# The last layer's gate columns of the modulation: the sum over weight blocks made by VectorE instead of TensorE

## What is computed

```python
s_lat = jax.nn.silu(c)
s_ctx = jax.nn.silu(c_ctx)
for l in range(DEPTH_2):
    last = l == DEPTH_2 - 1
    ...
    shift, scale, gate = jnp.split((s_lat @ w_mod[l] + b_mod[l])[:, None, :], 3, axis=-1)
    shift_c, scale_c, gate_c = jnp.split(s_ctx @ w_mod[l] + b_mod[l], 3, axis=-1)
    ...
    if not last:
        ...
        ctx = ctx + gate_c * y_c
    x = x + gate * y
```

## Time and profile before

| what | us |
|---|---|
| median of 3 runs | 2725.45 |
| lowest and highest run | 2723.93, 2725.97 |
| profiled execution | 2726.38 |
| its span | 2724.6 |
| TensorE busy | 2705.9 |
| VectorE busy | 1775.1 |
| ScalarE busy | 1299.4 |
| GpSimd busy | 337.6 |

### The profile page before, as it was taken

One profiled execution on the slowest core, in us unless ns is written; L12 is line 12 of the kernel. 1 busy time (PEld: TensorE's weight loads), 2 busy tenths in 40 slices (PEclk: granted clock), 3 DMA queues, 4 the chain that ended last, 5 costly groups with the idle time before them and its releaser, 6 DMA issues.

```text
span 2724.6 us, 32623 instructions
## 1 busy us (share of the span) xinstructions
PE 2705.9 (99%) x13110; PEld 2138.1 (78%) x13110; DVE 1775.1 (65%) x2386; ACT 1299.4 (48%) x1896; POOL 337.6 (12%) x309
## 2 busy tenths in 40 slices
PE   9999999999999999999999999999999999999998
PEld 7677777778877777777777887888778888877787
DVE  4737757765666666565646664758976665788765
ACT  4454445554544444344534444555556454555554
POOL 0000100000031010001010300224300111332001
PEclk9999999999999999999999999999999999999999
DMA  9878575465678776777877766665445656554553
GB/s 308 297 272 306 172 256 178 159 236 195 226 269 302 254 248 225 256 261 262 289 243 264 258 213 212 197 223 181 140 141 198 208 184 204 173 170 140 171 185 138
DMA packets 293191, 600.32 MB, mean 220 GB/s; under 512 B 12562, under 2 KB 19418, under 8 KB 291120
## 3 DMA queue, kind: packets, MB, share of 16 engines
q1 hardware_dynamic: 279856, 547.81, 58.7%
q0 software_dynamic: 10656, 46.94, 4.6%
q10 hardware_dynamic: 2528, 3.49, 0.4%
HBM read 585.02 MB, written 13.17 MB: 220 GB/s over the span
## 4 chain that ended last, share of the span: by engine, by line
PE 96%; DVE 2%; DMA 1%; issue 0%; ACT 0%; SPq 0%; DVEq 0%; ACTq 0%
PE ps L716 28%; PE ps L718 27%; PE ps L717 27%; PE ps L764 3%; PE ps L1232 1%; PE ps L1192 1%; DMA raw<-in_w_in_dram 1%; PE ps L696 1%; PE ps L955 1%; DVE wlo L1974 1%; PE ps L1066 1%; PE ps L1027 1%; PE ps L1200 1%; PE ps L1290 1%; PE ps L1314 1%; PE ps L992 0%
## 5 line engine op out<-in xcount | busy, mean ns | idle before, releaser
L1974 DVE TENSOR_TENSOR wlo<-raw,whi 128x1024 fp32r<-128x1024 f32 x834 | 1051.3, 1287 | 712.3 <-ACT whi L1402 707.9
L1402 ACT ACTIVATE whi<-raw 128x1024 fp32r<-128x1024 f32 x834 | 865.5, 1056 | 1075.2 <-PE ps L718 715.4
L716 PE MATMUL ps<-whi,ay_hi 128*128 128x512 f32 x1712 | 683.5, 399 | 1.2 <-DVE zsc L2278 1.2
L718 PE MATMUL ps<-whi,ay_lo 128*128 128x512 f32 x1712 | 667.9, 390 | 0.0
L717 PE MATMUL ps<-wlo,ay_hi 128*128 128x512 f32 x1712 | 667.1, 390 | 0.0
L716 PE MATMUL ps<-whi,ax_hi 128*128 128x512 f32 x1600 | 639.3, 400 | 1.7 <-DVE wlo L1974 1.7
L718 PE MATMUL ps<-whi,ax_lo 128*128 128x512 f32 x1600 | 624.2, 390 | 0.0
L717 PE MATMUL ps<-wlo,ax_hi 128*128 128x512 f32 x1600 | 623.4, 390 | 0.0
L716 PEld LDWEIGHTS ps<-whi,ay_hi 128*128 128x128 f32 x1712 | 322.0, 188 | 84.3 <-issue 17.8
L718 PEld LDWEIGHTS ps<-whi,ay_lo 128*128 128x128 f32 x1712 | 321.3, 188 | 68.9
L716 PEld LDWEIGHTS ps<-whi,ax_hi 128*128 128x128 f32 x1600 | 300.5, 188 | 95.4 <-issue 28.1
(11 more groups left out here) (524 smaller groups left out, 1992.6 us busy)
## 6 DMA issues: line engine op xcount, KB each, us to landing
raw<-in_w_in_dram SPq DMA_DIRECT2D x207, 1024.0 KB, 5.2
raw<-in_mlp_w_dram SPq DMA_DIRECT2D x128, 1024.0 KB, 6.9
raw<-in_w_mod_dram SPq DMA_DIRECT2D x96, 1024.0 KB, 9.2
raw<-in_w_out_dram SPq DMA_DIRECT2D x64, 1024.0 KB, 5.1
raw<-in_ple_gate_dram SPq DMA_DIRECT2D x16, 1024.0 KB, 5.1
z2c<-zsc POOLq DMA_DIRECT2D x13, 512.0 KB, 4.0
G<-bias_d ACTq DMA_DIRECT2D x4, 768.0 KB, 6.5
h<-in_ctx_dram POOLq DMA_DIRECT2D x1, 2048.0 KB, 8.2
```

Source lines behind the costliest of these rows:

```text
L716: mm(dst, hi_[:, kk, tt], whi[:, x.s % 2, k, :], start=(nth == 0), stop=False)
L718: ins = mm(dst, lo_[:, kk, tt], whi[:, x.s % 2, k, :], start=False, stop=(nth == KT - 1))
L1402: A(part(whi[:, x.s % 2], x, kh), part(raw[:, x.slot], x, kh), ACT.Copy).then_inc(hi_ready, 1)
L1974: V.tensor_tensor(part(wlo[:, x.s % 2], x, kh), part(raw[:, x.slot], x, kh), f32v(part(whi[:, x.s % 2], x, kh)), ALU.subtract).then_inc(lo ...
```

## The change

The four gate chunks of the last layer (`SUMS`, m = 12 to 15, G12 to G15) are no longer multiplied by TensorE. VectorE reads each of their blocks from its slot of `raw` and adds up over the 16 groups of 128 weight rows: the weights times the latent condition's value of that row, into one tile `modp_b` of 128 partitions by 512 columns (`mod_sum`). It is called behind the low parts of the units with at = 1, 2, 4 and 5, one block each, and then frees the slot. Behind the unit with at = 0 of the next seven TensorE adds the 128 partitions with one matmul of ones, and ScalarE copies the row at at = 2 of those seven, three units later than before. VectorE's three row additions go for these chunks, and POOL's store moves to i = (7m + 16) // 4 + 1 and waits for the copy. Only the latents' row is computed; the context's row, which nothing reads, holds the same numbers. What is loaded, and in which order, stays.

```diff
+SUM_AT = (1, 2, 4, 5)
...
+        SUMS = [m_ for m_, (l, col) in enumerate(MODB) if l and col >= MODSS]
...
-                if 0 <= m_ < len(MODB) and at in (1, 4):
+                if at == 0 and m_ - 1 in SUMS:
+                    pe.wait_ge(plain_used, MOD1[4 * m_ - 1].p + 1)
+                    pe.wait_ge(ev("modc_set"), MODSS + len(COLS))
+                    pe.wait_ge(ev("mod_row"), len(ROWS) - len(SUMS))
+                    pe.wait_ge(ev("mod_part"), before(ROWS, m_ - 1))
+                    mm(ps[0:32, 3, :], ones[:, 0:32], modp_b, start=True, stop=True).then_inc(ev("modc_sum"), 1)
+                if 0 <= m_ < SUMS[0] and at in (1, 4):
...
                 k = before(ROWS, m_)
-                act.wait_ge(plain_used, y.p + 1)
+                if m_ in SUMS:
+                    act.wait_ge(ev("modc_sum"), MODSS + len(COLS) + before(SUMS, m_) + 1)
+                else:
+                    act.wait_ge(plain_used, y.p + 1)
...
-                if at == 6 and m_ in ROWS:
+                if at == 6 and m_ in ROWS and m_ not in SUMS:
                     mod_row(m_, MOD1[4 * m_ + 3])
+                if at == 2 and m_ - 1 in SUMS:
+                    mod_row(m_ - 1, MOD1[4 * m_ - 1])
...
+            def mod_sum(m_, y):
+
+                dve.wait_ge(raw_in[y.slot], y.landed)
+                dve.wait_ge(plain_used, y.p)
+                if y.u == 0:
+                    dve.wait_ge(ev("modc_sum"), MODSS + len(COLS) + before(SUMS, m_))
+                for k in range(UK):
+                    w, c_ = raw[:, y.slot, k], cvec[:, UK * y.u + k, 0:1]
+                    if y.u == 0 and k == 0:
+                        ins = V.tensor_scalar(modp_b, w, c_, None, ALU.mult)
+                    else:
+                        ins = V.scalar_tensor_tensor(out=modp_b, in0=w, scalar=c_, in1=modp_b, op0=ALU.mult, op1=ALU.add)
+                    if k < UK - 1:
+                        link(ins)
+                ins.then_inc(plain_used, 1)
...
-                if at == 6 and m_ in ROWS:
+                if m_ in SUMS and at in SUM_AT:
+                    mod_sum(m_, MOD1[4 * m_ + SUM_AT.index(at)])
+                if at == 6 and m_ in ROWS and m_ not in SUMS:
                     mod_row(m_)
...
-                    if i == (7 * m_ + MOD1_AT + 8) // 4 + 1:
+                    if i == (7 * m_ + MOD1_AT + (12 if m_ in SUMS else 8)) // 4 + 1:
                         l, col = MODB[m_]
                         k = before(ROWS, m_)
-                        pool.wait_ge(ev("mod_row"), k + 1)
+                        if m_ in SUMS:
+                            pool.wait_ge(ev("mod_part"), k + 1)
+                        else:
+                            pool.wait_ge(ev("mod_row"), k + 1)
```

## The result

The changed kernel takes 2735.4 us (median of 7 runs, 2734.3 to 2737.0), the kernel before 2726.0 beside it: ratio 1.0036, 95% interval 1.0026 to 1.0046, so 9.4 us are lost. The forecast was 2730.0, no change close to its upper edge; the time lies inside the range, 5.4 above the forecast. By the bound of 0.2% that the prediction sets for no change, +0.36% is slower. The profiled execution took 2736.95 us with a span of 2735.1. Of its 10.5 us over the span before, 1.0 lies ahead of the MLP (unit 0 starts at 730.00 instead of 729.03), which the change does not touch.

What follows compares the result with a forecast made beforehand. The prediction took TensorE to bound the kernel and summed -16.8 + 3.6 + 2.5 + 0.9 + 10.9 + 2.0 + 1.4 = +4.5 us to a forecast of 2730 us, range 2720 to 2738.

Runs made afterwards that it cites:

- f5: The best kernel (f3) with one edit undone, the ones matmul again one unit later: 2722.3 us.
- f3: f2 with the sums of steps 92, 96, 100 and 104 again ahead of the evacuation, the best kernel: 2714.8 us.
- e2: The changed kernel with the sums of steps 92, 96, 100 and 104 behind the evacuation instead of ahead of it: 2726.4 us.
- e3: The changed kernel with both POOL's gate-row stores one turn earlier and the four sums behind the evacuations: 2725.9 us.
- e4: The changed kernel with one of the four chained instructions of each sum, three quarters of the products left out: 2721.0 us.
- e5: e3 plus TensorE's ones matmul of each chunk one unit earlier: 2722.2 us.
- f2: e5 plus the context branch's products one step later and each sum ahead of that branch's work of its step: 2717.2 us.
- f4: f2 with the stores of the gate rows again late, behind the squares: 2717.4 us.
- e7: The changed kernel with each of the four ones matmuls issued twice, one execution: 2737.2 us.
- e1: The changed kernel with POOL's four gate-row stores one turn of its loop earlier, ahead of the squares: 2726.2 us.
- e6: The changed kernel with the ones matmul one unit earlier and nothing else: 2730.2 us.
- after: The changed kernel itself, without follow-up edits, against the kernel before: 2735.4 us, ratio 1.0036.
- f6: The changed kernel with two edits only, stores one turn earlier and the ones matmul one unit earlier: 2722.0 us.

## What to carry to other kernels

Where work moves to an engine that runs ahead of the bound one, list all that the bound engine takes from it, buffers handed back as well as data, and look at what will now stand directly in front of each. Look also for the one tile that ties the moved work to the bound engine's own progress: here, with the other edits in place, 37 us more on VectorE cost 5.6 us of waiting with the tile released one unit late (f5), and 0.5 with it released in time (f3). A busy share says little on this; the fastest of these kernels has the busiest VectorE.

## What the runs showed of the hardware

**A small store takes longer while large transfers are under way.** The gate rows' 4 KB stores landed in 1.6 us (1.61 to 1.65) in each of the nine cases with no weight block under way when they were issued (in e2, e3, e4, e5, f2 and f4). With two blocks under way they took 2.8 to 5.8, and landed within 0.6 us of the second block, but for one in e7 (1.0). The stores of the earlier trace rows are such a mix; their median of 5.5 came near the 5.3 of this case, where two blocks were under way, and would have been far off in e2. The Trainium skill, DMA: Bandwidth & Descriptors, "Anatomy of one DMA — SWDGE (gpsimd) path", gives a fixed cost of about 2.0 us. The stores with no block under way, 1.6, lie 0.4 below that, and those with two under way lie above it. The last store of each run takes 10.8 to 11.8 in all kernels; why was not tried.

**The same wait may or may not lower the clock.** Unit 94's wait of 2.1 to 2.2 us was followed by a stretch of 3.4 us at the 1.2 GHz level in four of the eight kernels that have it (e1, e2, e3, e6) and by none in four (after, e5, e7, f6). Each of these cost 1.6. What decides between them, these rows do not tell; that it need not be the edit shows e1, which does what after does until its first moved store, at 1389.2, and has the dip at 1345.6. What such a stretch costs goes with what TensorE does in it: 6.85 us at 0.50 cost 2.1 in after, with TensorE busy for 4.15 of them behind its wait of 7.2, and 3.0 in e2 behind a wait of only 3.0 at unit 105, with TensorE busy for 6.11.

**POOL and VectorE hold each other up.** Two squares take 2.04 with nothing but an evacuation beside them and 3.02 beside low parts; a sum beside two squares took 4.12 instead of 3.11 in e2, about one square of 1.0 more. The Trainium skill, SBUF — State Buffer, "SBUF: two separate sides", describes a port pair shared by the two engines that one holds for a whole instruction. The sum's loss, 1.0 against 1.04 for one square, agrees with that; no run here shows the port itself.
